# First attention of a hybrid DiT kernel: sums of squares as two rounded passes, projections half a step sooner

## The reference, cut to what matters

```
def rmsnorm(x, g):
    xf = x.astype(jnp.float32)
    y = xf * lax.rsqrt(jnp.mean(xf * xf, axis=-1, keepdims=True) + EPS)
    return (y * g.astype(jnp.float32)).astype(x.dtype)

q = rmsnorm((rmsnorm(h[..., :256], cq_g) @ w_uq).reshape(B, L, 12, 96), q_g)
k = rmsnorm(concat[kv[..., :64], k_rope], k_g)
s = concat[q @ k_ctx, q @ k] * 96 ** -0.5 ;  o = softmax(s) @ v
```

## Time and profile before

| | us |
|---|---|
| median of three runs | 3051.41 |
| profiled execution, its own time | 3050.67 |
| its span | 3048.9 |
| first head prepared alone (to its first scores) | about 250 to 290 |
| the twelve heads | about 290 to 850 |
| TensorE busy over the span | 2911.8 (96%) |
| VectorE, ScalarE, GpSimd busy | 1811.4, 1349.0, 702.6 |

### The profile page before, as it was taken

The page is one execution under the profiler, slowest core; times in us unless marked ns, Lnnn a source line. Parts: engine busy times, 40 slices in busy tenths (PEclk is TensorE's granted clock), DMA queues, the critical chain, the costliest instruction groups (busy, mean ns, idle before and its releaser), DMA issues. The chain is left out here.

```text
span 3048.9 us, 38038 instructions
## 1 busy us (share of the span) xinstructions
PE 2911.8 (96%) x13994; PEld 2106.6 (69%) x13994; DVE 1811.4 (59%) x2476; ACT 1349.0 (44%) x2138; POOL 702.6 (23%) x509
## 2 busy tenths in 40 slices
PE   5998999999999999999999999969999999999999
PEld 2563444444478888889998887834548788888887
DVE  5124655556536888888863444346653878887442
ACT  4014565655624444446652432136662544445231
POOL 0002555555610233330000000034550133331000
PEclk9998999999999999999999999979999999999999
DMA  9920000000030222225664431032211122224453
GB/s 380 375 93 2 5 3 4 4 2 2 7 117 29 83 83 83 83 83 175 189 206 126 143 102 49 35 73 65 59 46 48 64 83 83 83 83 148 137 171 100
DMA packets 101750, 282.86 MB, mean 93 GB/s; under 512 B 12129, under 2 KB 27745, under 8 KB 94562
## 3 DMA queue, kind: packets, MB, share of 16 engines
q1 hardware_dynamic: 101602, 280.88, 28.4%
HBM read 237.97 MB, written 27.26 MB: 87 GB/s over the span
## 5 line engine op out<-in xcount | busy, mean ns | idle before, releaser
L1370 ACT ACTIVATE z_wh<-part 128x512 fp32r<-128x512 f32 x266 | 166.3, 629 | 337.1 <-PE PS L1241 194.3
L1746 DVE TENSOR_TENSOR z_wdl<-part,z_wdh 128x512 fp32r<-128x512 f32 (+3 forms) x208 | 148.8, 721 | 256.5 <-ACT z_wdh L1423 256.3
L1241 PE MATMUL PS<-s_uh,z_wl 128*128 128x512 f32 x736 | 286.6, 389 | 0.0
L1240 PE MATMUL PS<-s_ul,z_wh 128*128 128x512 f32 x736 | 286.5, 389 | 0.0
L1239 PE MATMUL PS<-s_uh,z_wh 128*128 128x512 f32 x736 | 286.4, 389 | 0.0
L1423 ACT ACTIVATE z_wdh<-part 128x512 fp32r<-128x512 f32 (+3 forms) x208 | 135.3, 655 | 303.1 <-DMA part<-in_w_down 302.0
L2403 POOL TENSOR_TENSOR X<-X 128x1024 f32<-128x1024 f32 x96 | 229.3, 2388 | 63.1 <-ACT X L2629 62.2
L1667 DVE TENSOR_TENSOR z_wl<-part,z_wh 128x512 fp32r<-128x512 f32 x266 | 218.4, 833 | 34.4 <-ACT z_wh L1370 34.4
L1226 POOL TENSOR_TENSOR part<-part,part 128x512 f32<-128x512 f32 x38 | 56.5, 1487 | 775.1 <-DMA part<-in_w_up 775.1
L2629 ACT ACTIVATE X<-PS 128x512 f32<-128x512 f32 x252 | 145.0, 593 | 143.0 <-PE PS L2425 135.6
L2725 DVE TENSOR_REDUCE part<-PS 128x1 f32<-128x512 f32 (+1 forms) x312 | 161.8, 579 | 17.1 <-PE PS L2528 16.3
(11 more groups left out here) (410 smaller groups left out, 7565.9 us busy)
## 6 DMA issues: line engine op xcount, KB each, us to landing
part<-in_w_up SPq DMA_DIRECT2D x132, 512.0 KB, 3.6
part<-in_mod_w SPq DMA_DIRECT2D x48, 1024.0 KB, 7.4
part<-in_w_down SPq DMA_DIRECT2D x96, 256.0 KB, 2.7
gated<-part SPq DMA_DIRECT2D x44, 512.0 KB, 2.6
part<-gated SPq DMA_DIRECT2D x87, 256.0 KB, 5.2
part<-in_w_down SPq DMA_DIRECT2D x32, 384.0 KB, 3.1
part<-in_w_down SPq DMA_DIRECT2D x32, 320.0 KB, 3.2
part<-in_w_down SPq DMA_DIRECT2D x48, 192.0 KB, 2.4
```

Source lines behind the costliest of these rows:

```text
L1240: pe.matmul(bank_, w_h, x_l, start=False, stop=False, skip_group_check=further)
L1241: return pe.matmul(bank_, w_l, x_h, start=False, stop=stop, skip_group_check=further)
L1370: act.activation(wh[i][:, :], full[b][i], ACT.Copy).then_inc(s["hi"], 1)
L1746: dve.tensor_tensor(wdl[j][:, :width(e)], wd[j][:, :width(e)], wdh[j][:, :width(e)].bitcast(F32), ALU.subtract).then_inc(s["wdl"], 1)
```

## The change

The squares are split into a high part rounded to fp32r (`skh`, `sqh`, by ScalarE) and a remainder (`skl`, `sql`, by VectorE, a subtraction of two tensors in SBUF), and `squares` adds two fp32r products where it had one fp32 product. `prep` now starts at half-step 1, so `project(n)` comes one half-step sooner; `squares`, `inverse` and `unit` of w now stand in `prep` w+2 and `high` and `low` in `prep` w+3. `prep` 8, at half-step 9, holds `high(5)` and `low(5)`. Two projections go to other banks, `sq` and `t1` trade places in SBUF, and there is a preamble for the constant rows.

```
@@ buffers
-            raw, sq = [[Xf[...] for n in range(2)] for x in range(2)]
-            t1 = [take(BANK) for _ in range(2)]
+            raw, t1 = [[Xf[...] for n in range(2)] for x in range(2)]
+            sql = [place(f"h0_sql{n}", o + n * BANK, BANK) for n in range(2)]
+            sq = [take(BANK) for _ in range(2)]
+            sqh = [place(f"h0_sqh{n}", 9088 + n * BANK, BANK) for n in range(2)]
+            skh, skl = place("h0_skh", ..., T), place("h0_skl", ..., T)
+            unity = place("h0_unity", 10 * A_HEADS * 64, A_QK)
-            PB = [RB, TB, RB, TB, RB, RB]
+            PB = [RB, RB + 1, RB, TB, RB, TB]
@@ steps_at
-                    if 2 <= v <= 8:
-                        return [("prep", v - 2)]
+                    if 1 <= v <= 8:
+                        return [("prep", v - 1)]
                     if 9 <= v <= 16:
-                        return [("prep", 7)] * (v == 9) + [("max", v - 9)]
+                        return [("prep", 8)] * (v == 9) + [("max", v - 9)]
@@ tensor: project
-                        elif w == 1:
+                        elif w in (2, 4):
+                            pe.wait_ge(s["sq"], 6 * p + w - 1)
+                        elif w == 3:
                             at_least(pe, "fin", p - 1)
                         elif w == 5:
-                            pe.wait_ge(s["sq"], 6 * p + 5)
-                            pe.wait_ge(s["ts"], 2 * p + 2)
-                        else:
-                            pe.wait_ge(s["sq"], 6 * p + (w - 1 if w < 5 else w))
+                            pe.wait_ge(s["sq"], 6 * p + 4)
+                            pe.wait_ge(s["ts"], 2 * p + 1)
@@ tensor: squares
-                        pe.wait_ge(s["sq"], 6 * p + w + 1)
+                        pe.wait_ge(s["sql"], 6 * p + w + 1)
+                        if w == 0:
+                            pe.wait_ge(s["sq"], 6 * p + 2)
                         at_least(pe, "lo", 6 * p + w - 1)
-                        pe.matmul(ps(NB[w % 2], ...), ones[0:A_QK, 0:A_QK], src, start=True, stop=True)
+                        for x in (skh, skl) if w < 3 else (sqh[w % 2], sql[w % 2]):
+                            mm = pe.matmul(ps(NB[w % 2], ...), unity[0:A_QK, :], part, start=..., stop=...)
@@ tensor: step            (scalar: high n-3, inverse n-2, project n)
-                            if n < 6:
-                                project(p, b, use, n)
-                            if 0 < n < 7:
-                                squares(p, n - 1)
+                            if 1 < n < 8:
+                                squares(p, n - 2)
+                            if n < 6:
+                                project(p, b, use, n)
@@ scalar: project, behind the Square (keys; the same for queries with sqh)
+                            act.wait_ge(s["sq"], 6 * p + w + 1)
+                            act.activation(skh[0:64, lo:hi], sk[0:64, lo:hi], ACT.Copy).then_inc(s["sqh"], 1)
@@ scalar: preamble
+                    act.activation(skh[64:96, :], sk[64:96, :], ACT.Copy).then_inc(s["kh0"], 1)
+                    act.activation(unity[:, :], ones[:, 0:A_QK], ACT.Copy).then_inc(s["kh0"], 1)
@@ vector
+                    def square_low(p, w):
+                        dve.wait_ge(s["sqh"], 6 * p + w + 1)
+                        ...
+                        dve.tensor_tensor(out_, in_, h_.bitcast(F32), ALU.subtract).then_inc(s["sql"], 1)
@@ vector: step
-                        if kind == "prep" and n > 1:
-                            low(p, b, n - 2)
+                        if kind == "prep" and n > 2:
+                            low(p, b, n - 3)
+                        if kind == "prep" and 1 < n < 8:
+                            unit(p, b, n - 2)
                         if kind == "prep" and 3 <= n < 5:
                             turn(p, n)
-                        if kind == "prep" and 0 < n < 7:
-                            unit(p, b, n - 1)
+                        if kind == "prep" and n < 6:
+                            square_low(p, n)
@@ vector: preamble, ahead of the five memsets
+                    dve.wait_ge(s["kh0"], 1)
+                    dve.tensor_tensor(skl[64:96, :], sk[64:96, :], skh[64:96, :].bitcast(F32), ALU.subtract)
```

More of the change, by code:

```diff
@@ L2277, in heads0 @@
             rest += 2 * T
-            raw, sq = [[Xf[:, rest + (2 * x + n) * BANK:rest + (2 * x + n + 1) * BANK] for n in range(2)] for x in range(2)]
-            t1 = [take(BANK) for _ in range(2)]
+            raw, t1 = [[Xf[:, rest + (2 * x + n) * BANK:rest + (2 * x + n + 1) * BANK] for n in range(2)] for x in range(2)]
+            sql = [place(f"h0_sql{n}", o + n * BANK, BANK) for n in range(2)]
+            sq = [take(BANK) for _ in range(2)]
+            sqh = [place(f"h0_sqh{n}", 9088 + n * BANK, BANK) for n in range(2)]
             lnb = take(BANK)
@@ L2283, in heads0 @@
             osb = take(BANK + P)
+            skh, skl = place("h0_skh", O_MIX + 5 * T, T), place("h0_skl", -(-o // 32) * 32, T)
+            unity = place("h0_unity", 10 * A_HEADS * 64, A_QK)
             rope = ROPE
@@ L2305, in heads0 @@
                      ("one", "one1", "pad", "pad1", "S", "P", "PV", "raw", "rawc",
-                      "sq", "nt", "ln", "rinv", "t1", "ts", "ta", "out", "hi", "lo", "cast", "vs", "mx", "mc", "mn", "mrow",
+                      "sq", "sqh", "sql", "kh0", "nt", "ln", "rinv", "t1", "ts", "ta", "out", "hi", "lo", "cast", "vs", "mx", "mc", "mn", "mrow",
                       "mr", "o", "bc", "lnr", "rs", "fin", "ad")}
@@ L2502, in squares @@
                         lo, hi = CH[w % 3]
-                        pe.wait_ge(s["sq"], 6 * p + w + 1)
+                        pe.wait_ge(s["sql"], 6 * p + w + 1)
+                        if w == 0:
+                            pe.wait_ge(s["sq"], 6 * p + 2)
                         at_least(pe, "lo", 6 * p + w - 1)
-                        src = sk[0:A_QK, lo:hi] if w < 3 else sq[w % 2][0:A_QK, :hi - lo]
-                        pe.matmul(ps(NB[w % 2], hi - lo, slice(0, A_QK)), ones[0:A_QK, 0:A_QK], src,
-                                  start=True, stop=True).then_inc(s["nt"], 1)
+                        for x in (skh, skl) if w < 3 else (sqh[w % 2], sql[w % 2]):
+                            part = x[0:A_QK, lo:hi] if w < 3 else x[0:A_QK, :hi - lo]
+                            mm = pe.matmul(ps(NB[w % 2], hi - lo, slice(0, A_QK)), unity[0:A_QK, :], part,
+                                           start=x in (skh, sqh[w % 2]), stop=x in (skl, sql[w % 2]))
+                        mm.then_inc(s["nt"], 1)
                     def step(kind, n, p, b, use):
                         if kind == "prep":
+                            if 1 < n < 8:
+                                squares(p, n - 2)
                             if n < 6:
                                 project(p, b, use, n)
-                            if 0 < n < 7:
-                                squares(p, n - 1)
                         if kind == "max" and n < 8:
@@ L2587, in project @@
                                 .then_inc(s["sq"], 1)
+                            act.wait_ge(s["sq"], 6 * p + w + 1)
+                            act.activation(sqh[w % 2][0:96, :n], sq[w % 2][0:96, :n], ACT.Copy).then_inc(s["sqh"], 1)
                     def inverse(p, w):
@@ L2610, in step @@
                         if kind == "prep":
-                            if n > 1:
-                                high(p, b, n - 2)
+                            if n > 2:
+                                high(p, b, n - 3)
+                            if 1 < n < 8:
+                                inverse(p, n - 2)
                             if n < 6:
                                 project(p, n)
-                            if 0 < n < 7:
-                                inverse(p, n - 1)
                         if kind == "row":
@@ L2703, in turn @@
                                                  op0=ALU.mult, op1=ALU.mult).then_inc(s["ts"], 1)
+                    def square_low(p, w):
+                        lo, hi = CH[w % 3]
+                        n = hi - lo
+                        dve.wait_ge(s["sqh"], 6 * p + w + 1)
+                        if w < 3:
+                            out_, in_, h_ = skl[0:64, lo:hi], sk[0:64, lo:hi], skh[0:64, lo:hi]
+                        else:
+                            out_, in_, h_ = [x[w % 2][0:96, :n] for x in (sql, sq, sqh)]
+                        dve.tensor_tensor(out_, in_, h_.bitcast(F32), ALU.subtract).then_inc(s["sql"], 1)
                     def low(p, b, w):
@@ L2731, in step @@
                             dve.tensor_scalar(mcb[:, 8:10], mc[:, 24:26], -1.0, None, ALU.mult).then_inc(s["mn"], 1)
+                    dve.wait_ge(s["kh0"], 1)
+                    dve.tensor_tensor(skl[64:96, :], sk[64:96, :], skh[64:96, :].bitcast(F32), ALU.subtract).then_inc(s["kh0"], 1)
                     for n, x in enumerate((kh[1], kl[1], qh[1], ql[1])):
```

## The result

Four runs of the changed kernel took 3091.16 to 3094.87 us, median 3092.39; the four of the kernel before beside them 3046.3 to 3053.41, median 3049.59. The ratio is 1.0141 (95% interval 1.0123 to 1.0159): slower by 42.8 us. Forecast were +25.6 us and at most 3090. The direction was right, the size too small, and the range missed.

What follows compares the result with a forecast made beforehand. A head was taken as bounded by when VectorE's reductions start, plus a fixed rest. First head 5.8 plus 19.8 us over 11 heads gave +25.6 on 3050.67: 3076 us, range 3054 to 3090.

Steps and rivals of the forecast that it cites:

- What bounds a head: Head length is the time from `spread` until VectorE's reductions start, 26.65 us before the change, plus a rest.
- plus a fixed rest: After the reductions start, the remainder of a head was taken as constant, so only the start would move.
- The collision: GpSimd's addition of unit 4 holds VectorE's low part of chunk 4: +1.8 us a head, 19.8 over 11 heads.
- two cases: Addition of unit 4 begins first, reductions at 28.5 (+1.9); or low part of chunk 4 first, 28.3 (+1.65).
- With nothing in the way 0 to +0.25: Without a hold by GpSimd, a head's reductions would start at 26.65 to 26.9, 0 to +0.25 us a head.
- TensorE's 2.4 us become waiting: The 2.4 us a head saved by cheaper passes becomes waiting before `squares(0)`, `(4)`, `(5)` and the first `max`.
- The first head +5.8: In the head prepared alone, constant-row work and chunk 0's new steps delay `unit(0)` by 5.8 us; bounds +4.3 to +7.
- the three kinds of room: Rivals around the forecast: no collision (chance 0.14), faster by the half-step (0.11), a second subtraction held a head (0.13).
- the half-step pays: From `squares(0)` to `unit(1)`, an earlier chain returns TensorE's 2.4 us a head: 3030 us, or 3043 for half; chance 0.11.

Runs made afterwards that it cites:

- with the collision cleared: Changed kernel with GpSimd's addition of unit 4 held until VectorE's second rotation sum, the cast of chunk 3 put before it: 3056.41 us, ratio 1.001.
- The kernel filled at three places: Changed kernel plus 9, 4 and 5 unused fp32r products a head, before squares of chunks 4 and 5 and the second max group: 3075.95 us, ratio 1.0068.
- the order alone: Changed kernel without the split: new order and banks, fp32 squares, no copies, subtractions or preamble; 3056.97 us, ratio 1.0013.

## Why the prediction was wrong

- *What bounds a head* (first reduction after the `spread`, plus a rest): right in its form in every kernel. But "plus a fixed rest" is the step that failed. In the kernel before and the changed one the rest has two values, 20.8 and 22.4 us, by whether TensorE's clock falls in it to the lower level (0.50 in the row at 438 us, 1.2 GHz) for some 3.4 us. It was in the trace of before, in two heads of ten, 49.0 and 49.1 us long among 47.4; I laid out a single head and took it for all. With 5.7 us of waits a head it falls there in nine of ten, wholly or in part.
- *The collision*: right, in place, mechanism and size. Forecast: low part of chunk 4 wanted at 18.25, addition from 18.10 to 20.45, end 21.0, reductions at 28.5. Measured: 18.32, 18.13 to 20.47, 21.02, 28.68. The term was set at +1.8 a head by leaning to the middle of two cases; it is +2.1, so 23.1 us for 19.8. The hold of chunk 1 was not in the layout, and happened to cost nothing. That the trace before has no pair of a one-input GpSimd instruction and such an operation was read wrong: at 192.41 two operations on SBUF tensors (line 2205) took 1.28 us beside a memset from 192.46 to 193.62, and 1.28 at 193.67 without one.
- *With nothing in the way 0 to +0.25*: right; +0.05 with the collision cleared.
- *TensorE's 2.4 us become waiting*: right (3.8 us in front of `squares`), but none of it in front of `max`, where the waits went from 14.5 to 12.9 us over ten heads. What that waiting costs beyond itself was left out, and that is the clock's term.
- *The first head +5.8*: 4.6 in the profiled execution of the changed kernel; 5.6 in four other kernels with the same preamble (30.7 or 30.8 against 25.2). Within its bounds. `unit(0)` came 6.1 us later for the 5.8 laid out, and from there to the first reduction it took 16.8 us, for 18.25 before and the 17 at least that I had; why, stays open.
- *Range and rivals*: the three kinds of room that I allowed were all in VectorE's chain. With the clock's term, 1.03 us a head between the two traces (11.3 us for eleven), the sum is 25.6 + 3.3 + 11.3 = 40.2; the traces show 8.3 + 31.3 = 39.6 up to the last `spread`, and the last 3 us to the 42.8 between the medians lie outside these heads and aren't explained. The kernel filled at three places ran at 3075.95 us. That this is the predicted time is partly luck: against the kernel before beside it (3055.61) it is +20.3 us, for the +25.6 forecast. The rival that the half-step pays was wrong as written, but the order without the split and without the collision does gain 14.6 us between medians.

## What to carry to other kernels

Before adding an operation with two SBUF operands to VectorE, or moving one, lay its start and GpSimd's instructions on one time line. A half-step's move put an unchanged operation on an addition, which held it for 2.2 us, 1.8 of which reached the reductions (27.93 against 26.17 with the addition moved); curing one collision by a delay made the next. Saved TensorE work that ends as waiting can cost twice: ask of each added wait what the clock does behind it and which engine is the limit there (the same fall cost 1.6 us in the rest and nothing in front of the reductions), and look at more than one period of a loop for a second length of the same work. And a saving on one engine is worth what the reductions' start says, not what its own row says.

## What the runs showed of the hardware

- A GpSimd cast, with one input, holds VectorE too: the low part of chunk 3 at 421.19 took 0.78 us with the cast beside it ending at 421.42, 0.55 before the end of the subtraction. In the order alone a rotation sum at 362.38 took 1.03 for 0.68, with a cast from 362.26 to 362.86. A GpSimd memset doesn't: the subtraction of 1280 columns at 256.57, beside one, took 1.48 us, and 2.89 for two without GpSimd. The Trainium skill (GPSIMD Engine Reference, Key points) names contention with two-input VectorE instructions and no GpSimd kind; this trace agrees for additions and casts, and not for memsets.
- The holding is complete, not a sharing: in the six places of 512 columns that I read, the held operation ended 0.55 to 0.56 us after GpSimd's instruction, in the two of 256 columns 0.28 after it. Most of its own time (0.55 of 0.69, 0.28 of 0.42) lies behind. Who begins first decides: 0.01 us in one head of the order alone turned it round.
- Idle time of TensorE in a head is no exact measure of the fall of its clock. The order alone (fp32 squares) waited 3.6 us a head, and its clock never fell in ten heads. With nine products filled in, the changed kernel waited 3.7 and its clock fell in 6 of 10. With the collision cleared it waited 3.9 and its clock fell in 2 of 10, as in the kernel before with 2.4. What separates them stays open.
